# Doubling an unmasked triangular system and masking its product in ScalarE's copy, with new places for the read-back, the gate differences, the spread and the convolutions

## The reference

```python
dn_qkv = jax.nn.silu(causal_dwconv(dn_qkv, dn_conv_w))        # width 4, before q, k, v
g = jnp.cumsum(g, axis=-1)
decay = jnp.where(causal, jnp.exp(jnp.where(causal, g_i - g_j, 0.0)), 0.0)
L = jnp.where(strict, (k_beta @ k.T) * decay, 0.0)
T_mat = triangular_solve(eye + L, eye, lower=True, unit_diagonal=True)
u, w = T_mat @ v_beta, T_mat @ (k_beta * exp(g))
def step(S, ...):                                             # over the chunks
    v_new = u_i - w_i @ S
    o = qd_i @ S + qa_i @ v_new
    S = S * exp(g_last) + kt_i.T @ v_new
```

## Time and profile before

| | |
|---|---|
| runs, us | 1250.89, 1251.06, 1254.26 |
| profiled execution, us | 1252.81 |
| its span, us | 1251.1 |
| PE busy | 1226.1 us, 98% |
| DVE busy | 877.2 us, 70% |
| ACT busy | 738.8 us, 59% |
| POOL busy | 214.9 us, 17% |
| granted TensorE clock, mean | 0.997 |

### The profile page before, as it was taken

How to read it: one execution, slowest core, us unless ns; L and a number is a source line. 1 busy time by engine, 2 the same in 40 slices (tenths; PEclk the granted TensorE clock), 3 DMA queues, 4 the chain that set the end, 5 groups by cost and what they waited for, 6 DMA issues and landing times.

```text
span 1251.1 us, 20175 instructions
## 1 busy us (share of the span) xinstructions
PE 1226.1 (98%) x6651; PEld 1051.1 (84%) x6651; DVE 877.2 (70%) x1633; ACT 738.8 (59%) x1454; POOL 214.9 (17%) x254
## 2 busy tenths in 40 slices
PE   8899999999999999999999999999999999999997
PEld 6787897889888888788888888888888888888886
DVE  5878866754444754788878888887887885555554
ACT  7767558544867555666566656656656554444442
POOL 1120511141103000022222322222232220000000
PEclk9999999999999999999999999999999999999999
DMA  9647332842443655255455455555555565555551
GB/s 375 254 154 244 138 127 92 251 140 103 148 154 135 218 188 200 103 202 199 173 199 198 168 201 182 189 189 184 195 183 193 194 236 186 186 200 203 185 185 67
DMA packets 35909, 228.91 MB, mean 183 GB/s; under 512 B 6528, under 2 KB 6928, under 8 KB 9232
## 3 DMA queue, kind: packets, MB, share of 16 engines
q1 hardware_dynamic: 34016, 223.50, 50.2%
q10 hardware_dynamic: 1840, 4.71, 1.2%
HBM read 225.96 MB, written 2.24 MB: 182 GB/s over the span
## 4 chain that ended last, share of the span: by engine, by line
PE 85%; DVE 5%; ACT 3%; DMA 3%; issue 2%; POOL 1%; SPq 1%; DVEq 0%; ACTq 0%; POOLq 0%
PE bank L1334 32%; PE bank L1338 16%; PE bank L1362 10%; PE bank L1360 10%; PE bank L1361 10%; DVE w_lo L896 2%; DMA arena<-in_x_tok 2%; DMA arena<-base_rows 1%; DVE arena L917 1%; PE bank L1479 1%; ACT w_hi L464 1%; PE bank L1472 1%; PE bank L1455 1%; PE bank L1639 1%; PE bank L1637 1%
## 5 line engine op out<-in xcount | busy, mean ns | idle before, releaser
L896 DVE TENSOR_TENSOR w_lo<-raw,w_hi 128x512 fp32r<-128x512 f32 x816 | 574.8, 726 | 263.6 <-ACT w_hi L464 259.3
L464 ACT ACTIVATE w_hi<-raw 128x512 fp32r<-128x512 f32 x816 | 502.2, 630 | 356.3 <-PE bank L1334 176.8
L1334 PE MATMUL bank<-xhl,w_hi 128*128 128x512 f32 x2044 | 659.7, 399 | 5.4 <-DVE arena L901 2.7
L1338 PEld LDWEIGHTS bank<-xhl,w_lo 128*128 128x128 f32 x2044 | 384.8, 188 | 88.0
L1338 PE MATMUL bank<-xhl,w_lo 128*128 128x256 f32 x2044 | 402.4, 278 | 0.0
L1334 PEld LDWEIGHTS bank<-xhl,w_hi 128*128 128x128 f32 x2044 | 317.1, 189 | 7.3 <-DVE w_lo L896 3.3
L1361 PE MATMUL bank<-w_lo,ffn_act 128*128 128x512 f32 x336 | 130.7, 389 | 0.0
L1360 PE MATMUL bank<-w_hi,ffn_act 128*128 128x512 f32 x336 | 130.7, 389 | 0.0
L1362 PE MATMUL bank<-w_hi,ffn_act 128*128 128x512 f32 x336 | 130.7, 389 | 0.0
L434 POOL TENSOR_TENSOR arena<-arena,token_scale 128x256 f32<-128x256 f32 x88 | 78.1, 902 | 302.9 <-DVE arena L901 192.5
L1258 DVE SCALAR_TENSOR_TENSOR arena<-arena,fcw 128x256 f32<-128x256 f32 x176 | 85.3, 485 | 23.9 <-DVE arena L1255 1.5
(11 more groups left out here) (239 smaller groups left out, 1005.6 us busy)
## 6 DMA issues: line engine op xcount, KB each, us to landing
raw<-in_wts SPq DMA_DIRECT2D x203, 1024.0 KB, 4.8
xfeat<-in_x SPq DMA_DIRECT2D x4, 512.0 KB, 8.6
arena<-in_x_tok SPq DMA_DIRECT2D x1, 2048.0 KB, 19.8
xfeat<-in_x_tok SPq DMA_DIRECT2D x1, 2048.0 KB, 9.2
arena<-base_rows ACTq DMA_DIRECT2D x4, 512.0 KB
out_y<-xfeat SPq DMA_DIRECT2D x8, 256.0 KB, 2.0
arena<-gate_rows SPq DMA_DIRECT2D x1, 1024.0 KB, 4.2
arena<-in_post_gains ACTq DMA_DIRECT2D x1, 1024.0 KB, 6.1
```

Of the source, the lines that this page charges most:

```text
L464: nc.scalar.activation(w_hi[:, i % RING, :], raw[:, slot, quarter * PIECE:(quarter + 1) * PIECE], ACT.Copy).then_inc(hi_ready, 1)
L896: V.tensor_tensor(w_lo[:, i % RING, :], raw[:, slot, quarter * PIECE:(quarter + 1) * PIECE], w_hi[:, i % RING, :].bitcast(f32), ALU.subtra ...
L1334: return M(ps[j][:, :], w_hi[:, r % RING, kk * P:(kk + 1) * P], xhl[:, k, :, :].rearrange("p a t -> p (a t)"), start=(k == 0), stop=(k == ...
L1338: return M(ps[j][:, 0:T], w_lo[:, r % RING, kk * P:(kk + 1) * P], xhl[:, CHUNK_K * q + kk, 0, :], start=False, stop=False, skip_group_chec ...
```

## The change

The changed kernel no longer masks `ltri` on POOL. `x_mm` multiplies the whole triangular matrix, and ACT masks the product while it copies it: for each block of columns one activation whose scale is a column of ones and zeros over partitions (`row_mask`), four in level 0, two in level 1, one in level 2. The other half of the columns of `xb` is set to zero by a memset on POOL (`x_zero`), for which `y_mm` waits. The masks of the attention (`tri`, `neg1`) get their own room and are made at the start.

The spread of the 16x16 solution goes from POOL to DVE, at places 69 and 70 in batch 0 instead of 72, and `turn` comes one place earlier. The read-back is issued by SP directly behind the stores and waits there for them. The gate differences and the exponential of batch 1 move from places 100 to 104 into the last steps of batch 0 (places 92 to 95 on DVE, and on ACT between `qs` and `z1`). The convolutions of groups 4 to 6 end three places earlier, their SiLU too. Four steps of the prologue stand one place later. `WARM` is 7 instead of 8. At the two ends, `out_tile` and `down_tile` of the last tile come behind the first residual instead of before it.

```diff
-WARM = 8
+WARM = 7
...
+MASK_AT = [0, 4, 6, 7]
...
-SILU_AT = [10, 9, 10, 15, 15, 15]
-CONV_AT = [(3, 5, 7, 9)] + [(1, 3, 5, 7)] * 2 + [(1, 5, 9, 13)] * 3
+SILU_AT = [10, 9, 10, 12, 12, 12]
+CONV_AT = [(3, 5, 7, 9)] + [(1, 3, 5, 7)] * 2 + [(1, 4, 7, 10)] * 3
...
-PLACE = {"ba": 10, "stat": 14, "ba_turn": 16, "scale": 15, "gate": 21, "gcum": 24, "grow": 28}
+PLACE = {"ba": 10, "stat": 15, "ba_turn": 17, "scale": 16, "gate": 21, "gcum": 25, "grow": 28}
...
-        PLACE["spread", _b, _g] = _l + 35
-        PLACE["turn", _b, _g] = _l + 37 + _g
+        PLACE["spread", _b, _g] = _l + 32 + _g
+        PLACE["turn", _b, _g] = _l + 36 + _g
     PLACE["store", _b] = _l + 6
-    PLACE["load", _b] = _l + 11
-    for _i in range(4):
-        PLACE["dm", BH * _b + _i] = _l - 3 + _i
-    PLACE["dexp", _b] = _l + 1
...
+for _i in range(BH):
+    PLACE["dm", _i] = 34 + _i
+    PLACE["dm", BH + _i] = 92 + _i
+PLACE["dexp", 0], PLACE["dexp", 1] = 39, 98
...
+                sp.wait_ge(s("scratch_in"), 16 * NBLK * (b + 1))
+                for jh in range(2):
+                    rows_ = slice(jh * BASE // 2, (jh + 1) * BASE // 2)
+                    sp.dma_start(block_l[:, rows_].rearrange("p j u i -> p (j u i)"),
+                                 scratch[b].rearrange("(n j) (o x) -> n o j x", j=BASE, o=1)[:, :, rows_, :].rearrange(
+                                     "n o j x -> n o (j x)").to_broadcast([NBLK, BASE, BASE * UNITS * BASE // 2])
+                                 ).then_inc(s(f"block_in{jh}"), 16)
...
+            step(pool.memset(row_mask, 1.0))
...
-            def level_b(i):
+            def x_zero(i):
                 b, r = divmod(i, 2 * LEVELS)
                 lv, g = divmod(r, 2)
                 follow(PLACE["x", i] - 2)
                 if r < 2:
                     pool.wait_ge(s("base_row"), BASE * (b + 1))
-                if i >= 2:
-                    pool.wait_ge(s("x_mm"), i - 1)
-                pool.tensor_tensor(bb[:, g, :, :], ltri[:, 4 * g:4 * g + 4, :], each(lmask[:, lv, :]), ALU.mult
-                                   ).then_inc(s("b_ready"), 1)
+                else:
+                    pool.wait_ge(s("y_mm"), i - 1)
+                pool.memset(half_columns(xb[:, g, :, :], lv, 1), 0.0).then_inc(s("x_zero"), 1)
...
+            def decay(b):
+                follow(PLACE["dexp", b] - 1)
+                act_e.wait_ge(s("ddiff"), BH * b + BH)
+                lot = dm[:, BH * b:BH * b + BH, :]
+                nc.scalar.activation(lot, lot, ACT.Exp).then_inc(s("dexp"), 1)
+
             for b in range(BATCHES):
                 h0 = BH * b
-                follow(PLACE["dexp", b] - 1)
-                act_e.wait_ge(s("ddiff"), h0 + BH)
-                nc.scalar.activation(dm[:, h0:h0 + BH, :], dm[:, h0:h0 + BH, :], ACT.Exp).then_inc(s("dexp"), 1)
+                if b == 0:
+                    decay(0)
...
-                follow(PLACE["load", b])
-                act_e.wait_ge(s("scratch_in"), 16 * NBLK * (b + 1))
-                for jh in range(2):
-                    rows_ = slice(jh * BASE // 2, (jh + 1) * BASE // 2)
...
-                    nc.scalar.activation(xb[:, i % 2, :, :], ps[4][:, :] if i % 2 == 0 else ps[5][:, :], ACT.Copy
-                                         ).then_inc(s("x_sb"), 1)
+                    lv = i % (2 * LEVELS) // 2
+                    w = BASE << lv
+                    product = ps[4 + i % 2].rearrange("p (u n) -> p u n", n=P)
+                    for m in range(MASK_AT[lv], MASK_AT[lv + 1]):
+                        c = slice(2 * w * (m - MASK_AT[lv]), 2 * w * (m - MASK_AT[lv]) + w)
+                        ins = nc.scalar.activation(xb[:, i % 2, :, c], product[:, :, c], ACT.Copy,
+                                                   scale=row_mask[:, m:m + 1])
+                    ins.then_inc(s("x_sb"), 1)
...
+                if b == 0:
+                    decay(1)
...
+            def gate_difference(b):
+
+                for h in range(BH * b, BH * b + BH):
...
+                dve.wait_ge(s("base_row"), BASE * (b + 1))
+                for g in range(2):
+                    follow(PLACE["spread", b, g])
+                    V.tensor_tensor(
...
+                if b == 0:
+                    gate_difference(1)
...
-                out_tile(NB - 1, j)
...
-            dve.wait_ge(s("m_evac"), NJ * NB)
             hidden(1, 0)
+            out_tile(NB - 1, 1)
             hidden(1, 1)
...
                 inverse(stat[:, 2, j:j + 1])
-                down_tile(NB - 1, j)
                 dve.wait_ge(s("row_root"), j + 5)
-                dve.wait_ge(s("f_evac"), NJ * (NB - 1) + j + 1)
+                dve.wait_ge(s("f_evac"), NJ * (NB - 1) + j)
                 for c in range(NB):
+                    if c == 1:
+                        down_tile(NB - 1, j)
+                    if c == NB - 1:
+                        dve.wait_ge(s("f_evac"), NJ * (NB - 1) + j + 1)
                     residual(down, 2, j, c * 512, (c + 1) * 512, "y_ready")
...
-                pe.wait_ge(s("b_ready"), i + 1)
...
-                    last = M(ps[4 + g][:, u * P:(u + 1) * P], bb[:, g, u, :], tmat[:, 4 * g + u, :],
+                    last = M(ps[4 + g][:, u * P:(u + 1) * P], ltri[:, 4 * g + u, :], tmat[:, 4 * g + u, :],
...
+                pe.wait_ge(s("x_zero"), i + 1)
...
-                pe.wait_ge(s("tri_ready"), 2)
+                pe.wait_ge(s("tri_ready"), 1)
```

More of the change, by code:

```diff
@@ L160, in hybrid_block_kernel @@
         dm = cut(HEADS * T).rearrange("p (h t) -> p h t", t=T)
-        lmask = cut(LEVELS * P).rearrange("p (l n) -> p l n", n=P)
+        tri = cut(P)
+        neg1 = cut(P)
+        row_mask = cut(P)[:, 0:7]
         pos_block = cut(P)
@@ L325, in _ @@
                                     pattern=[[BASE, NBLK], [0, BASE]], channel_multiplier=-1))
+            step(pool.memset(row_mask, 1.0))
             for lv in range(LEVELS):
                 w = BASE << lv
+                m = row_mask[:, MASK_AT[lv]:MASK_AT[lv + 1]]
                 na = P // (2 * w)
[L329 to L336 removed]
+                step(pool.affine_select(out=m, in_=m, compare_op=ALU.is_ge, fill=0.0, base=-w,
+                                        pattern=[[-2 * w, na]], channel_multiplier=1))
+                step(pool.affine_select(out=m, in_=m, compare_op=ALU.is_ge, fill=0.0, base=2 * w - 1,
+                                        pattern=[[2 * w, na]], channel_multiplier=-1))
+            step(pool.memset(tri, -1.0))
+            step(pool.affine_select(out=tri, in_=tri, compare_op=ALU.is_ge, fill=0.0, base=0,
+                                    pattern=[[-1, P]], channel_multiplier=1))
+            pool.memset(neg1, -1.0).then_inc(s("tri_ready"), 1)
             at = [-1]
@@ L395, in _ @@
                                    pattern=[[0, UNITS], [1, P]], channel_multiplier=-1).then_inc(s("dmask"), 1)
-                for g in range(2):
-                    follow(PLACE["spread", b, g])
-                    pool.wait_ge(s("base_row"), BASE * (b + 1))
-                    pool.tensor_tensor(
-                        tmatT[:, 4 * g:4 * g + 4, :].rearrange("p u (b i) -> p u b i", i=BASE),
-                        base_cols[:, 4 * g:4 * g + 4, :].rearrange("p u (o i) -> p u o i", o=1).to_broadcast([P, 4, NBLK, BASE]),
-                        pos_block.rearrange("p (o b i) -> p o b i", o=1, i=BASE).to_broadcast([P, 4, NBLK, BASE]),
-                        ALU.mult).then_inc(s("spread"), 1)
                 for i in range(2 * LEVELS * b, 2 * LEVELS * (b + 1)):
-                    level_b(i)
+                    x_zero(i)
             follow(SB_PLACE - 1)
-            pool.wait_ge(s("b_ready"), 2 * LEVELS * BATCHES)
-            step(pool.memset(lmask[:, 0, :], -1.0))
-            pool.memset(lmask[:, 1, :], -1.0).then_inc(s("tri_ready"), 1)
-            pool.affine_select(out=lmask[:, 0, :], in_=lmask[:, 0, :], compare_op=ALU.is_ge, fill=0.0, base=0,
-                               pattern=[[-1, P]], channel_multiplier=1).then_inc(s("tri_ready"), 1)
             for h in range(BH):
@@ L1009, in _ @@
             V.tensor_copy(grow, ps[6][0:ALL_UNITS, 2 * P:3 * P]).then_inc(s("grow_sb"), 1)
-            for b in range(BATCHES):
-                h0 = BH * b
-                for h in range(h0, h0 + BH):
+            def gate_difference(b):
+                for h in range(BH * b, BH * b + BH):
                     follow(PLACE["dm", h])
@@ L1019, in _ @@
                     ins.then_inc(s("ddiff"), 1)
+            for b in range(BATCHES):
+                h0 = BH * b
+                if b == 0:
+                    gate_difference(0)
                 follow(PLACE["kt", b, 1] + 2)
@@ L1059, in _ @@
                                     mybir.AxisListType.X, ALU.add).then_inc(s("base_row"), 1)
+                dve.wait_ge(s("base_row"), BASE * (b + 1))
+                for g in range(2):
+                    follow(PLACE["spread", b, g])
+                    V.tensor_tensor(
```

(5 more changed lines are left out.)

15 lines of the change are left out of this document (2 added, 13 removed).

## The result

The changed kernel took 1257.59 us (median of 7 runs, 1256.88 to 1258.80), the kernel before 1252.57 (median of 7, 1250.89 to 1255.52). The ratio is 1.004 (95% interval 1.0027 to 1.0052): some 5 us slower, where 1246.2, 4.9 us faster, had been forecast. The new wait stands where the forecast put one, but it is 7.46 us long and not 3.5, and TensorE runs at half clock for a while behind it.

A forecast was written before the change was run, and what follows sets the result against it. PE was busy 1226.1 of 1251.1 us, so only its waits, 11.1 us together, could give. Terms -1.39 - 1.14 - 2.75 + 3.5 - 0.22 - 1.7 - 0.9 - 0.4 + 0.1 = -4.9: 1246.2 us, range 1241.5 to 1251.5.

The forecast's parts named there:

- The read-back: Batch 0: chunk 15 queued behind SP's read-back makes the SiLU late; new PE wait at the transposes of v, +3.5 us.
- D: Time the read-back flows in SP's queue ahead of chunk 15; taken as 6.3 us, midway between 4.2 and 8.5.
- 95.0 + 6.3 + 2.4: Chunk 15's landing: read-back flows from about 95.0 us, for 6.3, then 2.4 for the chunk.
- the first rival: Chunk 15 isn't held up behind the read-back in SP's queue; the 3.5 us are gone, 1242.7 us; chance 0.25.
- The slow read-back: Rival: transfers keep their pace beside the chunks; longer PE wait at batch 0's transposes of v, 1257 to 1259; chance 0.08.
- Prologue: PE's waits for the token scales (-1.39 us) and the gate column (-1.14) shrink as steps move one piece later.
- Transposes of q: Batch 0: with the read-back out of ACT's order, PE's wait of 2.75 us there goes, -2.75.
- Doublings: PE's two waits for POOL's masked matrix go, -1.7 us; ACT's split-up copies and POOL's memset are covered.
- `turn`: PE's wait there goes, -0.22 us, with the spread on DVE and `turn` a piece earlier.
- the forecast's cover: At `turn`: DVE's two products, about 0.65 us each, replace POOL's 3.36 us spread and cover `turn` standing a piece earlier.
- Group 7: 206 to 216 us: first `added` 0.2 later, second freed-bank wait of 1.09 gone; sum -0.9 us, bounds -2.74 and +1.8.
- Ends: First residual comes 0.4 us earlier, -0.4; at the program's end DVE idles for the root, +0.1.

The follow-up runs named there:

- Experiment 3: Kernel before with only the read-back moved to SP, directly behind the stores: 1259.05 us, ratio 1.006 to the kernel before.
- 1: Changed kernel with the read-back put back into ScalarE's order at place 48: 1249.84 us, ratio 0.9985 to the kernel before.
- 2: Changed kernel with chunks 15 and 16 issued on SP between the stores and the wait for them: 1249.71 us, ratio 0.9976 to the kernel before.
- experiment 13: Changed kernel, read-back DMAs reading 128 overlapping 4 KB rows of the same 64 KB of stored blocks (leading dimension 128): 1247.51 us, ratio 0.9955.
- 14: Changed kernel, read-back DMAs reading weights as 8 by 16 by 4 KB, no place read twice (leading dimension 8): 1257.24 us, ratio 1.0039.
- experiment 9: Changed kernel with 30 useless matmuls before TensorE's wait for the SiLU at batch 0's transposes of v: 1255.12 us, ratio 1.0015.
- experiment 4: Kernel before with the unmasked product, ScalarE's masks and POOL's memset alone; spread stays on POOL: 1250.18 us, ratio 0.9984.
- experiment 7: Kernel before with the four prologue places alone (stat 15, ba_turn 17, scale 16, gcum 25): 1250.98 us, ratio 0.9993.
- 6: Changed kernel with the read-back in ScalarE's order at place 50: 1250.08 us, ratio 0.9978 to the kernel before.
- experiment 8: Changed kernel, read-back on ScalarE at place 50, ba_turn, turn, groups 4 to 6 convolutions and SiLU at old places, gate-sum copy at 24: 1246.26 us, ratio 0.9955.
- Experiment 12: Changed kernel with the read-back on ScalarE at place 50 and groups 4 to 6 convolutions and SiLU at old places: 1248.22 us, ratio 0.9963.
- experiment 5: Changed kernel with the read-back as eight DMAs on SP, each one stored block to 16 partitions: 1254.04 us, ratio 1.0012.
- 11: Changed kernel with the read-back's two DMAs reading 512 KB each of weights, each partition from its own place: 1249.61 us, ratio 0.9973.

## Why the prediction was wrong, step by step

**The read-back (+3.5 forecast, +7.46 and a clock loss found): the step that failed.** It has two parts, the size of D and the clock. The structure held: queued behind SP's wait, chunk 15 late, then ScalarE's splits, squares and SiLU, and PE at the transposes of v. Experiment 3 makes the wait with this edit alone, 1 and 2 take it away in two different ways. What failed is the size of D. The forecast put it at 6.3, midway between sixteen engines (4.2) and eight (8.5); the packets ran from 93.2 to 103.8, 10.5 us. They began 1.8 earlier than assumed, ran 4.2 longer, and the chunk landed 3.5 behind them instead of 2.4, in all 3.6 later than 95.0 + 6.3 + 2.4. The 256 packets of 4 KB took 84.7 engine-us, which over 10.5 us is eight engines at work; experiments 13 and 14 show that it is the shape and not the source.

By the Trainium skill (DMA: Bandwidth & Descriptors, Why a DMA increments its semaphore by 16) eight was the number to take: the runs agree with it, and the midpoint was no value that either case gives. The other 2 us came beside chunk 15: alone a packet took 0.25 us (8.2 us for all on eight engines), but from 96.5 on, with packets of chunk 15 beside them, they took 0.4. The forecast reasoned that the read-back would have the engines to itself, and it had them for 3.3 us.

The sentence of the Trainium skill that the issuer only saves issue time (same page, Issuing engines are not separate DMA queues), which spoke for the first rival, is half borne out. Transfers of both issuers do share the engines: in the kernel before, a chunk issued at 96.24, beside ScalarE's read-back, took 12.8 us to land instead of 4.8.

```profile
raw<-in_wts SPq DMA_DIRECT2D x1, 1024.0 KB, 12.8
```

But which issuer has the read-back decides what stands behind it. With ScalarE's, SP issues chunk 15 at 90.20 and it lands in 5.3 us, before the read-back starts; with SP's, it is issued at 93.17 and lands 14.1 us later, at 107.3.

The slow read-back stood among the rivals with 0.08, and by its price the kernel was over 0.3% slower only with D above 15. At D = 10.5 the forecast's own sum still gives -0.7, so D alone doesn't make the loss. What the sum lacked besides:

**The clock, left out of the sum.** The forecast counted a wait of 3.5 us as 3.5. A wait of 7.46 cost 9.7, since PE worked at 0.50 for 4.8 us behind it; experiment 9 gives back 2.5 by keeping PE at work. With this part, the point from which the change loses lies lower than the text had it. Between the forecast's -4.9 and the +3.9 of the two profiles stand +4.0 of wait, +2.4 of clock, +1.6 of prologue, +0.4 of group 7 and the 0.35 at 87.8 us. A row that should have warned was in hand: the earlier trace rows shows such a dip behind the waits of 0.53 and 1.71.

**Prologue (-2.53 forecast, -0.95 found).** The first wait fell as forecast, to 0.63. The second was counted wrongly: the chain behind the gate column isn't fed late, but it isn't earlier either. DVE's last step of it, first in the kernel before and then after:

```profile
50.71 0.17 DVE L1001 SCALAR_TENSOR_TENSOR arena<-arena,gate 128x16 f32<-128x16 f32 x1
```

```profile
50.69 0.17 DVE L1004 SCALAR_TENSOR_TENSOR arena<-arena,gate 128x16 f32<-128x16 f32 x1
```

PE, a place earlier thanks to the scales, comes to it 1.39 us sooner and has one piece more to do: the two cancel, and both moves together are worth one piece and the 0.26 by which this wait fell, not 2.53. The new 0.70 at the transposes of the gate rows wasn't foreseen at all: `gcum` at place 25 puts a convolution ahead of DVE's copy.

```profile
54.62 1.52 DVE L920 SCALAR_TENSOR_TENSOR arena<-arena,dcw 128x255 f32<-128x255 f32 x3
56.06 0.17 DVE L1008 COPY arena<-bank 128x16 f32<-128x16 f32 x1
```

**Transposes of q (-2.75): right** as to the wait, which is gone. What that is worth depends on what TensorE met before. In experiment 4, which doesn't touch it, it was 1.51: the clock had dipped at 36 us in that execution, and TensorE came later. In experiment 7 it was 1.29, behind the 1.25 at 88.3.

**Doublings (-1.7): right**, by experiment 4. **`turn` (-0.22): right only by luck, because of the stall.** Where the stall is taken away (experiments 1, 2 and 6) it waits 0.55 to 1.5 us: the spread on DVE at the earlier place of `turn` costs more than the 0.22 that POOL's did, and the forecast's cover for it wasn't there. With `turn` back at its old place (experiment 8) there is no wait.

**Group 7 (-0.9 forecast, -0.5 found).** The second wait went as forecast; the first grew by 0.6 to 2.24 instead of 0.2. Experiment 12 separates the parts: with the gate differences and the exponential moved and the convolutions left, 1.08 remains of 2.74. By the waits, moving the first pays 1.7 and moving the second costs 1.2. The dip behind the longer wait (1.6 us) comes in some executions only: of the nine profiles with a wait of 2.2 there, six have it (the changed kernel, 2, 6, 9, 13 and 14) and three don't (1, 5 and 11). The same stretch in experiments 6 and 1:

```profile
210.80:214.20 3.40, 3.40 (x13) 2.81 (x12) 3.40 (x6) 1.08 (x3) 3.11 (x3) 0.50 0.16 21
209.30:213.00 3.70, 3.70 (x21) 3.26 (x22) 3.70 (x7) 2.01 (x5) 3.70 (x4) 1.00 0.13 13
```

Of the four with the old waits of 1.65 and 1.09 (before, 3, 4 and 7) none has it. With so few that isn't proof, but two thirds of 1.6, an estimate of 1 us, may be a further cost of the convolutions' new places. It would also fit experiment 12, which came out 0.8 below what its theory said.

**Ends (-0.3): right** by the trace: the wait for the residual is 0.19 shorter with one matmul of 0.23 less ahead of it, so the residual comes 0.4 earlier, as forecast. It is too small to be told from the time.

## What to carry to other kernels

Before a wait and a transfer are moved into a queue, price what stands behind them there with the number of engines that the transfer's shape gives (here eight) and with packets slowed by what runs beside them, and add what the clock takes from the work behind a long wait of TensorE. A wait on a chain that TensorE doesn't feed swallows what was gained ahead of it, so two such waits in a row are one gain and not two. When a large stall hides other costs, the parts must be judged with the stall taken away: here `turn` and group 7 looked free or cheap until then.

## What the runs showed of the hardware

In experiment 5, where each DMA reads one 8 KB block for 16 partitions, a packet of 8 KB took 1.00 us, where the chunks' take 0.31. Reads of overlapping places 480 bytes apart in the same 64 KB (experiment 13) had no such cost. Why the first are slow no run shows; that the engines read one block at one time is a guess.

Two transfers in one queue are not simply one behind the other. In the changed kernel packets of chunk 15 run from 96.5 us on, seven us before the read-back's last one, mostly 9 to 16 in a us and at 0.7 us each instead of 0.31, while the read-back's go from 0.25 to 0.4. Both lose, and the chunk still lands only 3.5 us after the read-back's end. Which engine carries which packet isn't in the trace, so why both slow down stays open.

The clock's dips behind waits of about 2 us come in some executions and not in others: behind the wait of 1.7 at the mixer's end in 12 of the 16 profiles, in group 7 as told above. Of the runs of the kernel before that the experiments list, the eleven with a mean granted clock of 0.998 took 1249.2 to 1252.2 us, the sixteen with 0.995 took 1252.6 to 1254.3. 0.003 of 1251 us is 3.8 us of lost clock, an estimate that would account for most of that spread. One profile does not say whether a given wait of 2 us will have a dip.
